# Order of products in a four-layer kernel: output tiles, a g tile inside the third mixer, a value tile, and small products between quarter tiles

## The chip, the core and the metric

One core of a Trainium2 chip runs the whole program in one launch. The metric is the device time of one execution in microseconds (us). TensorE (PE in the rows) multiplies, VectorE (DVE), ScalarE (ACT) and GpSimd (POOL) prepare its operands and take its results, and SyncE (SP) issues the loads of the weights from HBM.

## The reference, cut to what matters

Two models of two layers each run one after the other on one activation of 256 tokens by 1024 features, in float32.

```python
def fox_mixer(h, ...):      # attention, 16 heads of 64, with a forget gate of 16 columns
    q, k, v, f, z = split(h @ w_in);  log_f = log_sigmoid(f + b_f);  c = cumsum(log_f)
    ...
    return (o * silu(z)) @ w_out
def nsa_mixer(h, ...):      # q, kc, vc, ks, vs, kw, vw, gate, z = split(h @ w_in)
    kc = compress_blocks(kc_raw, pe_k, w_ck1, w_ck2)   # blocks of 32 tokens @ w1, silu, @ w2
    ...
    return (o * silu(z)) @ w_out
def _hgrn2_mixer(h, ...):   # third mixer: q, f, i, g = split(h @ w_in), 8 heads of 128
    o = _chunk_gated_recurrence(silu(q), 1 - forget, i, log(forget))
    return (_rmsnorm(o, out_norm) * silu(g)) @ w_out
...
def second_block(...):      # per layer: x += mixer(rmsnorm(x)); x += conv_ffn(rmsnorm(x))
```

The order is fox mixer, nsa mixer, hgrn mixer, FFN, MLA mixer, FFN.

## The kernel before, in words

**Weights.** All weights pass through a ring of three slots as tiles of 1 MB (128 partitions x 2048 float32). For each tile SP loads the ring slot, ACT writes the high part (`high`, line 385), DVE subtracts to get the low part (`low`, line 395, or in halves, line 404), and PE forms each product as three matmuls, high*high, low*high and high*low (`product3`, lines 421 to 423). SP may load tile t when the low part of tile t-3 is made; ACT may write the high part of tile t when PE has finished tile t-3. The list `tiles` sets the order, and every engine's program names the tiles in that order.

**A tile on PE.** `by_feature` and `by_token` do one tile as 2 halves (j) of 8 chunks (c) of 3 matmuls, 48 matmuls of 256 columns, into one of the PSUM banks 0 and 1, in turn. A bank is free when the tile two before it has been taken by DVE or ACT (`wait_bank`). `between(q)` is called after each quarter of a tile (4 chunks, 12 matmuls) and can put other products there. `ready(c)` waits for chunk c of the activations.

**Output projections.** `project_out` does the four tiles of the fox, nsa, hgrn and MLA output projections. In its first tile each chunk of half j=0 waits for `act_split`, the count of activation chunks that are split in high and low. In the fox, nsa and hgrn mixers the last two chunks come from the mixer's last z or g tile: DVE takes the bank, ACT applies tanh or silu, DVE multiplies, ACT writes the high part, DVE the low part (lines 1501, 1956, 2368).

**Fox.** The forget gate's product of 16 columns (`forget_product`, line 1391, 16 calls of two instructions each) is done at once in the middle of tile 1.

**NSA.** Tile order: kc, vc, ks, vs, kw, hk0, vw, hk1, q0, hv0, ... where hk and hv are the tiles of the compression's first product (`hidden`). They need the token blocks that DVE builds (`blocks`, line 1903, then the copy of line 1984 and the subtraction of line 1986, `block_split`) after eight DMAs have moved rows. DVE's order there is low(kw), wait for the DMAs, blocks(0), rope(0), blocks(1), high and low parts of the blocks, low(hk0), low(vw), low(hk1), rope(1), ... The second operation of rope(0) (line 1893) frees the bank of tile ks, which is the bank that kw needs.

**Third mixer.** After the f, q and i tiles comes a core of 8 heads. For each head PE sums exponents with the `levels` matrices (`exponents`, lines 2117 and 2119; w = 2*head + half, into banks 0 and 1 for an even w and 2 and 3 for an odd one), ACT takes exp (line 2221), DVE multiplies 8 levels (`mix`, line 2323), PE forms scores (`scores`, lines 2131 to 2139), DVE masks (2331) and adds levels (2339), PE forms outputs (`outputs`, lines 2150 to 2155, into bank 7 alone, one head after the other), ACT copies them out and squares them (2240, 2242). Then PE does g tile 0, 16 sums of squares (line 2171, each two instructions with one column), g tile 1, four spreads of the inverted roots (line 520), and g tiles 2 and 3.
DVE's queue behind g tile 1, in order: take g tile 1 (line 2269), norm and gate of parts 0 and 1, norm of parts 2 and 3 (line 2356; part i waits for spread i), low of output tile 0 (line 395), output_low(0) and (1) (line 2368), take g tile 2, gate(2), output_low(2), low of output tile 1, take g tile 3, gate(3), output_low(3). ACT's queue at its end: silu(2), output_high(2), high of output tile 1, silu(3), output_high(3).

## Time and profile before

| what | us |
|---|---|
| three runs | 1115.91, 1118.05, 1108.06 (median 1115.91) |
| the profiled execution's own time | 1112.2 |
| its span in the profile | 1110.4 |
| PE busy in the span | 1058.5 |
| DVE busy | 770.7 |
| ACT busy | 548.7 |

The profiled execution stands at 1112.2 us, of which 1.8 us lie around the span; it is 3.7 us below the median of the three runs. PE's busy time counts an engine that runs at half clock as fully busy, so the granted clock is read beside it.

### The profile page before, as it was taken

To read this page: it belongs to the slowest core of one execution; us is meant where nothing else is said; L and a number is where in the kernel's file an instruction comes from. 1 tells how busy PE (TensorE), PEld (TensorE's weight loads), DVE (VectorE), ACT (ScalarE), POOL (GpSimd) and SP (SyncE) were. 2 spreads that over 40 slices of the span, in tenths; PEclk is the share of its full clock that TensorE was granted. 3 is DMA by queue.
4 is the path that set the end of the run, shared out by engine and by line. 5 is a ranking of instruction groups with operands and counts; after the bars stand their busy time and mean duration, and the time that the engine had idled before them with its cause. 6 is when DMAs were issued, how large, how long until landed. Compare 5 with 4: busy or idle time off the path is not lost. (4 is left out here: it accounts for less than half of the span.)

```text
span 1110.4 us, 20549 instructions
## 1 busy us (share of the span) xinstructions
PE 1058.5 (95%) x8304; PEld 993.9 (90%) x8306; DVE 770.7 (69%) x1276; ACT 548.7 (49%) x862; POOL 76.5 (7%) x60
## 2 busy tenths in 40 slices
PE   7999999999998999899999999999899899999997
PEld 5988889897676999898989999999888799999997
DVE  5666666767676667477456887787677548887875
ACT  5544445355555545543355544454564455544451
POOL 4000005000000410000011000000300320000000
PEclk9899999999999999999999999999999999999999
DMA  8544335782112446400345666664323045755641
GB/s 265 152 120 147 115 117 171 223 265 75 39 39 77 149 155 194 148 1 7 104 130 141 190 193 178 195 188 144 120 76 115 19 134 153 216 171 180 189 152 39
DMA packets 176974, 152.31 MB, mean 137 GB/s; under 512 B 6845, under 2 KB 169220, under 8 KB 176900
## 3 DMA queue, kind: packets, MB, share of 16 engines
q1 hardware_dynamic: 176690, 151.22, 45.0%
q8 instruction: 52, 0.85, 0.3%
q14 instruction: 22, 0.18, 0.1%
q10 hardware_dynamic: 210, 0.05, 0.0%
HBM read 148.12 MB, written 1.05 MB: 134 GB/s over the span
## 5 line engine op out<-in xcount | busy, mean ns | idle before, releaser
L421 PE MATMUL bank<-h_high,w_high 128*128 128x256 f32 x1312 | 381.9, 291 | 6.2 <-DVE ffn_normed L1040 2.6
L422 PE MATMUL bank<-h_low,w_high 128*128 128x256 f32 x1312 | 374.0, 285 | 0.0
L423 PE MATMUL bank<-h_high,w_low 128*128 128x256 f32 x1312 | 373.8, 285 | 0.0
L385 ACT ACTIVATE w_high<-ring 128x2048 fp32r<-128x2048 f32 x138 | 263.3, 1911 | 189.1 <-PE bank L423 181.9
L395 DVE TENSOR_TENSOR w_low<-ring,w_high 128x2048 fp32r<-128x2048 f32 x119 | 273.4, 2300 | 32.6 <-ACT w_high L385 32.4
L421 PEld LDWEIGHTS bank<-h_high,w_high 128*128 128x128 f32 x1312 | 254.4, 194 | 13.5 <-issue 8.3
L422 PEld LDWEIGHTS bank<-h_low,w_high 128*128 128x128 f32 x1312 | 254.6, 194 | 0.7 <-issue 0.5
L423 PEld LDWEIGHTS bank<-h_high,w_low 128*128 128x128 f32 x1312 | 254.5, 194 | 0.0
L421 PE MATMUL bank<-ffn_hidden_high,w_high 128*128 (+1 forms) x352 | 99.8, 283 | 2.0 <-DVE ffn_hidden_low L1073 2.0
L422 PE MATMUL bank<-ffn_hidden_low,w_high 128*128 (+1 forms) x352 | 99.6, 283 | 0.0
L423 PE MATMUL bank<-ffn_hidden_high,w_low 128*128 (+1 forms) x352 | 99.6, 283 | 0.0
L568 POOL TENSOR_TENSOR h<-h 128x512 f32<-128x512 f32 x18 | 43.7, 2427 | 713.9 <-ACT h L552 713.3
L1049 DVE SCALAR_TENSOR_TENSOR ffn_conv<-ffn_normed,par,ffn_conv 128x254 f32<-128x254 f32 (+1 forms) x176 | 77.0, 479 | 7.4 <-ACT ffn_conv L1027 2.3
L1027 ACT ACTIVATE ffn_conv<-ffn_normed,par 128x256 f32<-128x256 f32 x88 | 48.0, 593 | 67.4 <-DVE ffn_normed L1040 67.2
L744 ACT ACTIVATE work<-bank,work 128x128 f32<-128x128 f32 (+1 forms) x112 | 46.2, 418 | 60.6 <-DVE work L729 60.5
L421 PEld LDWEIGHTS bank<-ffn_hidden_high,w_high 128*128 128x128 f32 x352 | 67.6, 192 | 2.3 <-issue 2.3
L423 PEld LDWEIGHTS bank<-ffn_hidden_high,w_low 128*128 128x128 f32 x352 | 67.6, 192 | 0.0
L422 PEld LDWEIGHTS bank<-ffn_hidden_low,w_high 128*128 128x128 f32 x352 | 67.6, 192 | 0.0
L729 DVE TENSOR_REDUCE work<-bank 128x2 f32<-128x256 f32 (+2 forms) x64 | 32.4, 507 | 40.0 <-PE bank L715 39.8
L710 PE MATMUL bank<-work 128*128 128x256 f32 (+2 forms) x160 | 53.2, 432 | 1.9 <-DVE work L2718 1.5
L404 DVE TENSOR_TENSOR w_low<-ring,w_high 128x1024 fp32r<-128x1024 f32 x38 | 46.1, 1220 | 7.1 <-ACT w_high L385 7.0
L421 PE MATMUL bank<-w_high,h_high 128*128 128x256 f32 x160 | 47.5, 297 | 2.9 <-DVE w_low L395 2.9
(344 smaller groups left out, 1823.9 us busy)
## 6 DMA issues: line engine op xcount, KB each, us to landing
ring<-in_ffn_w_up_dram SPq DMA_DIRECT2D x44, 1024.0 KB, 6.0
ring<-in_ffn_w_down_dram SPq DMA_DIRECT2D x22, 1024.0 KB, 5.0
ring<-in_fox_w_in_dram SPq DMA_DIRECT2D x16, 1024.0 KB, 5.7
ring<-in_hgrn_w_in_dram SPq DMA_DIRECT2D x16, 1024.0 KB, 5.5
ring<-in_nsa_w_in_dram SPq DMA_DIRECT2D x14, 1024.0 KB, 5.4
ring<-in_fox_w_out_dram SPq DMA_DIRECT2D x4, 1024.0 KB, 5.1
ring<-in_nsa_w_out_dram SPq DMA_DIRECT2D x4, 1024.0 KB, 5.1
ring<-in_hgrn_w_out_dram SPq DMA_DIRECT2D x4, 1024.0 KB, 5.2
```

Of the source, the lines that this page charges most:

```text
L385: i = nc.scalar.activation(dst, src, ACT.Copy)
L395: ops.tensor_tensor(w_lo[:, t % NSLOT, :], ring[:, t % NSLOT, :], w_hi[:, t % NSLOT, :].bitcast(F32), ALU.subtract).then_inc(low_in[t % NS ...
L404: i = nc.vector.tensor_tensor(w_lo[:, t % NSLOT, q], ring[:, t % NSLOT, q], w_hi[:, t % NSLOT, q].bitcast(F32), ALU.subtract)
L421: nc.tensor.matmul(o, ah, bh, start=start, stop=False, **kw)
L422: nc.tensor.matmul(o, ah, bl, start=False, stop=False, **kw)
L423: return nc.tensor.matmul(o, al, bh, start=False, stop=stop, **kw)
L568: nc.gpsimd.tensor_tensor(h[:, 0:2, :], h[:, 0:2, :], h[:, 2 * i:2 * i + 2, :], ALU.add).then_inc(n_added, 1)
L710: nc.tensor.matmul(o, q, k, start=(i == 0), stop=False)
L729: nc.vector.tensor_reduce(self.least[:, m, 0:unit["nh"]], self.bank(u), AX.X, ALU.min).then_inc(a_least, 1)
L744: i = nc.scalar.activation(pb[:, e, 0:unit["w"]], ps[:, e, :], ACT.Exp, scale=-1.0, bias=self.least[:, m, e:e + 1], accum_out=self.sum[:, ...
L1027: i = nc.scalar.activation(y[:, j % 2, e, :], un[:, j % 2, e, :], ACT.Identity, scale=column(cw + 4 * FC, e, j, later), bias=column(cb, e, ...
L1049: i = nc.vector.scalar_tensor_tensor(out=dst, in0=un[:, j % 2, e, 0:S - back], scalar=column(cw + (2 - back) * 2 * FC, e, j, later), in1=d ...
```

## The change

- Output tiles: a new `by_feature_late` does the first tile of each `project_out` with chunks 0 to 5 of half j=0, chunks 0 to 5 of half j=1, then chunks 6 and 7 of both.
- Fox: `forget_product` is cut in three parts of 6, 5 and 5 calls, put after quarters 0, 1 and 2 of tile 1.
- NSA: tile vw goes ahead of hk0 in the ring, on PE and on ACT. On DVE the low part of tile 5 of the mixer (now vw) goes ahead of the wait for the moved blocks; that of tile 6 (now hk0) stays behind the blocks, and that of tile 7 goes behind rope(1).
- Third mixer: at the start of the core w = 1 goes ahead of w = 0, only w = 0 waits for the banks of the i tiles, and ACT makes one small Exp ahead of its last i tile; every one of DVE's 8 multiplications of a head signals by itself, and each pair of score products waits for its own level; g tile 0 goes between the last scores and the outputs of heads 6 and 7; the sums of squares are cut in three parts after quarters 0, 1 and 2 of g tile 1; the four spreads go after the four quarters of g tile 2.

The queues of DVE and ACT behind the core are as before.

```diff
@@ -295,8 +295,8 @@
         nsa("ks", NSA_KS)
         nsa("vs", NSA_VS)
         nsa("kw", NSA_KW)
+        nsa("vw", NSA_VW)
         nsa_hidden("hk0", 0)
-        nsa("vw", NSA_VW)
         nsa_hidden("hk1", 1)
@@ -496,6 +496,21 @@
                         between(2 * tt + c // 4)
+        def by_feature_late(pe, t, act, ready):
+            in_parts(pe, t)
+            wait_bank(pe, t)
+            w = parts(t, "p (c n) -> p c n", c=DC, n=256)
+            for chunks in (range(DC - 2), range(DC - 2, DC)):
+                for j in range(2):
+                    for c in chunks:
+                        if j == 0:
+                            ready(c)
+                        mm = product3(pbank(t)[:, j * S:(j + 1) * S], [v[:, c, j * P:(j + 1) * P] for v in w],
+                                      [v[:, c, :] for v in act], (j, c) == (0, 0), c == DC - 1, skip_group_check=True)
+            mm.then_inc(tile_done, 1)
@@ -893,8 +908,9 @@
             first = first(nrm)
 
             def pe(pe):
-                for t in range(t0, t0 + 4):
-                    by_feature(pe, t, split, ready=(lambda c: pe.wait_ge(act_split, n0 + c + 1)) if t == t0 else None)
+                by_feature_late(pe, t0, split, lambda c: pe.wait_ge(act_split, n0 + c + 1))
+                for t in range(t0 + 1, t0 + 4):
+                    by_feature(pe, t, split)
                 first(pe)
                 nrm.sums(pe)
@@ -1384,20 +1400,19 @@
 
-                def forget_product():
+                def forget_product(part):
                     pe.wait_ge(w_f_ready, 1)
-                    for tt in range(TT):
-                        for c in range(DC):
-                            mm = nc.tensor.matmul(B[6][:, tt * FOX_H:(tt + 1) * FOX_H], x[:, c, tt * P:(tt + 1) * P],
-                                                  w_f[:, c, :], start=(c == 0), stop=(c == DC - 1))
-                    mm.then_inc(fps, 1)
+                    for i in range((0, 6, 11)[part], (6, 11, 16)[part]):
+                        tt, c = i // DC, i % DC
+                        mm = nc.tensor.matmul(B[6][:, tt * FOX_H:(tt + 1) * FOX_H], x[:, c, tt * P:(tt + 1) * P],
+                                              w_f[:, c, :], start=(c == 0), stop=(c == DC - 1))
+                    if part == 2:
+                        mm.then_inc(fps, 1)
 
                 def between(n, half):
 
-                    if (n, half) == (1, 0):
-                        forget_product()
                     if (n, half) == (2, 0):
                         c_sums()
                 def quarter(n, q):
                     if (n, q) == (1, 0):
                         nrm_fox.spread(pe)
+                    if n == 1 and q < 3:
+                        forget_product(q)
                     if q % 2:
                         between(n, q // 2)
@@ -1780,8 +1797,8 @@
                 by_feature(pe, NT2["ks"], hsp)
                 by_token(pe, NT2["vs"], hsp, between=rotate_after(0))
                 by_feature(pe, NT2["kw"], hsp)
+                by_token(pe, NT2["vw"], hsp, between=rotate_after(1))
                 hidden("hk0", 0, 0)
-                by_token(pe, NT2["vw"], hsp, between=rotate_after(1))
                 hidden("hk1", 0, 1)
@@ -1842,8 +1859,8 @@
                 evac_raw("ks", raw_k[0])
                 evac_values("vs", v2[0])
                 evac_raw("kw", raw_k[1])
+                evac_values("vw", v2[1])
                 hidden_in("hk0", 0, False)
-                evac_values("vw", v2[1])
                 hidden_in("hk1", 0, True)
@@ -1975,6 +1992,7 @@
                 lowest = pc("lower", 0, DC)
                 nc.vector.tensor_tensor(lower_exp[:, :], lowest, lowest, ALU.subtract).then_inc(lb_step, 1)
                 low(dve, nc.vector, t_in + 4)
+                low(dve, nc.vector, t_in + 5)
                 dve.wait_ge(moved_x, 128)
                 dve.wait_ge(nsa_cleared, XB_CLEAR)
                 blocks(0)
@@ -1985,10 +2003,9 @@
                 dve.wait_ge(block_high, 1)
                 nc.vector.tensor_tensor(b_lo[:, :, :], xb, b_hi[:, :, :].bitcast(F32),
                                         ALU.subtract).then_inc(block_split, 1)
-                for t in range(t_in + 5, t_in + 8):
-                    low(dve, nc.vector, t)
+                low(dve, nc.vector, t_in + 6)
                 rope(1)
-                for t in range(t_in + 8, t_in + 13):
+                for t in range(t_in + 7, t_in + 13):
                     low(dve, nc.vector, t)
                 rope(2)
                 low(dve, nc.vector, FIRST + 1)
@@ -2104,13 +2121,14 @@
                     by_token(pe, t_i + i, hsp)
                 pe.wait_ge(lf_split, 4)
                 pe.wait_ge(levels_in, 1)
-                evacuated(pe, t_i + 2)
-                evacuated(pe, t_i + 3)
 
                 def exponents(w):
                     hh, tt = w // 2, w % 2
+                    if w == 0:
+                        evacuated(pe, t_i + 2)
+                        evacuated(pe, t_i + 3)
                     if w >= 2:
-                        pe.wait_ge(decayed, w - 1)
+                        pe.wait_ge(decayed, max(2, w - 1))
                     for b in range(2):
                         c0 = 512 * (1 + tt) if b else 0
@@ -2123,14 +2141,15 @@
                 def scores(w):
                     hh, tt = w // 2, w % 2
                     tk = slice(tt * P, (tt + 1) * P)
-                    pe.wait_ge(mixed, hh + 1)
                     if w >= 2:
                         pe.wait_ge(masked, w - 1)
                     d = dec[:, hh % 2]
                     for l in range(MASKED):
+                        pe.wait_ge(mixed, (LEVELS + 1) * hh + l + 1)
                         nc.tensor.matmul(B[4 + tt][:, l * HD:(l + 1) * HD].rearrange("p (b i) -> p b i", i=1 << l),
                                          d[:, l, tk], halves(d[:, l, tk], l)[:, :, 1, :], start=True, stop=True)
                     nc.tensor.matmul(B[4 + tt][:, MASKED * HD:], keyT[:, hh, tk], qT[:, hh, tk], start=True, stop=True)
+                    pe.wait_ge(mixed, (LEVELS + 1) * (hh + 1))
                     if hh and not tt:
                         pe.wait_ge(cross_in, hh)
 
                 for k in range(HG_H + 2):
                     if k < HG_H:
-                        exponents(2 * k)
-                        exponents(2 * k + 1)
+                        exponents(2 * k + (k == 0))
+                        exponents(2 * k + (k > 0))
                     if 1 <= k <= HG_H:
                         scores(2 * k - 2)
                         scores(2 * k - 1)
+                    if k == HG_H:
+                        pe.wait_ge(decayed, NU)
+                        by_feature(pe, t_g, hsp)
                     if k >= 2:
                         outputs(k - 2)
 
-                by_feature(pe, t_g, hsp)
-                pe.wait_ge(sq_in, HG_H)
-                for k in range(NU):
-                    mm = nc.tensor.matmul(B[2][:, k:k + 1], sq8[:, k // 2, k % 2 * P:(k % 2 + 1) * P], ones[:, 0:1],
-                                          start=True, stop=True)
-                mm.then_inc(sq_ps, 1)
-                by_feature(pe, t_g + 1, hsp)
-                pe.wait_ge(o_inv, 1)
-                for i in range(4):
-                    spread(B[3 + i], [roots[:, k:k + 1] for k in range(4 * i, 4 * i + 4)]).then_inc(o_spread, 1)
-                by_feature(pe, t_g + 2, hsp)
+                def square_sums(q):
+                    pe.wait_ge(sq_in, HG_H)
+                    for k in range((0, 5, 10, NU)[q], (5, 10, NU, NU)[q]):
+                        mm = nc.tensor.matmul(B[2][:, k:k + 1], sq8[:, k // 2, k % 2 * P:(k % 2 + 1) * P],
+                                              ones[:, 0:1], start=True, stop=True)
+                    if q == 2:
+                        mm.then_inc(sq_ps, 1)
+                def spread_roots(q):
+                    pe.wait_ge(o_inv, 1)
+                    spread(B[3 + q], [roots[:, k:k + 1] for k in range(4 * q, 4 * q + 4)]).then_inc(o_spread, 1)
+                by_feature(pe, t_g + 1, hsp, between=square_sums)
+                by_feature(pe, t_g + 2, hsp, between=spread_roots)
                 by_feature(pe, t_g + 3, hsp)
                 out3_pe(pe)
@@ -2204,6 +2229,8 @@
                     half = slice(i % 2 * 512, (i % 2 + 1) * 512)
                     nc.scalar.activation(lf_hi[:, i // 2, half], B[2 + i][:, :], ACT.Copy).then_inc(lf_high, 1)
                 for i in range(4):
+                    if i == 3:
+                        nc.scalar.activation(scratch[:, :], eps[:, :], ACT.Exp)
                     act.wait_ge(tile_done, t_i + i + 1)
                     for tt in range(TT):
@@ -2214,7 +2241,7 @@
 
                 def exps(w):
                     hh, tt = w // 2, w % 2
-                    act.wait_ge(summed, w + 1)
+                    act.wait_ge(summed, w + 1 if hh else 2 - w)
@@ -2224,8 +2251,8 @@
 
                 for k in range(HG_H + 3):
                     if k < HG_H:
-                        exps(2 * k)
-                        exps(2 * k + 1)
+                        exps(2 * k + (k == 0))
+                        exps(2 * k + (k > 0))
                     if k == 1:
                         high(act, t_g + 2)
@@ -2320,8 +2347,7 @@
                     dve.wait_ge(decayed, 2 * hh + 2)
                     for l in range(LEVELS + 1):
                         d = halves(dec[:, hh % 2, l, :], l)
-                        i = nc.vector.tensor_tensor(d, d, sources(hh, l), ALU.mult)
-                    i.then_inc(mixed, 1)
+                        nc.vector.tensor_tensor(d, d, sources(hh, l), ALU.mult).then_inc(mixed, 1)
```

## Rows read from the trace of the kernel before

**Rows 1.** Page, part 1, busy time, share of the span and instructions of each engine

```profile
PE 1058.5 (95%) x8304; PEld 993.9 (90%) x8306; DVE 770.7 (69%) x1276; ACT 548.7 (49%) x862; POOL 76.5 (7%) x60
```

**Rows 2.** Windows: stretch, length, busy time (instructions) by engine, granted PE clock, DMA

```profile
31.99:37.80 5.81, 5.81 (x28) 5.81 (x29) 0.89 (x4) 2.08 (x4) 0.00 (x0) 0.50 0.56 172
460.90:475.00 14.10, 11.06 (x68) 9.10 (x68) 8.57 (x24) 10.08 (x17) 0.00 (x0) 1.00 0.22 75
640.00:660.00 20.00, 20.00 (x169) 20.00 (x168) 16.05 (x23) 8.96 (x10) 0.00 (x0) 1.00 0.69 199
```

**Rows 3.** Timeline of PE, first fox output tile: start, length, instruction, [idle before]

```profile
149.42 0.28 PE L421 MATMUL bank<-fox_out_high,w_high 128*128 128x256 f32 x1
...
151.43 0.27 PE L423 MATMUL bank<-fox_out_high,w_low 128*128 128x256 f32 x1
154.15 0.58 PE L421 MATMUL bank<-fox_out_high,w_high 128*128 128x256 f32 x1 [2.44 <-DVE fox_out_low L1501]
```

**Rows 4.** Waits of PE over the span: total us, times, longest

```profile
PE bank L421 <- DVE w_low L395: 5.7, 3, 2.9
...
PE bank L421 <- DVE blocks_low L1956: 3.4, 1, 3.4
...
PE bank L421 <- DVE hgrn_out_low L2368: 2.6, 1, 2.6
...
PE bank L421 <- DVE fox_out_low L1501: 2.4, 1, 2.4
...
PE bank L2131 <- DVE work L2323: 1.8, 1, 1.8
...
PE bank L421 <- POOL mla_out_low L439: 1.4, 1, 1.4
...
PE bank L2117 <- ACT work L2209: 1.0, 1, 1.0
PE bank L2150 <- DVE work L2339: 1.0, 1, 1.0
```

**Rows 5.** Groups of PE instructions: the forget product

```profile
L1391 PE MATMUL bank<-w_f,x 128*128 128x16 f32 x32 | 4.1, 276 | 0.0
```

**Rows 6.** Timeline of DVE in the NSA mixer, tiles ks to hk0

```profile
198.76 1.89 DVE L1903 TENSOR_TENSOR work<-work,par 128x480 f32<-128x480 f32 x2 [2.10 <-DMA work<-work]
...
201.16 0.68 DVE L1893 TENSOR_TENSOR work<-bank,work 128x512 f32<-128x512 f32 x1
...
205.83 2.29 DVE L1986 TENSOR_TENSOR blocks_low<-work,blocks_high 128x2048 fp32r<-128x2048 f32 x1
```

**Rows 7.** Timeline of ACT over the same stretch

```profile
196.34 1.90 ACT L385 ACTIVATE w_high<-ring 128x2048 fp32r<-128x2048 f32 x1
202.45 0.84 ACT L1808 ACTIVATE work<-bank,rstd 128x256 f32<-128x256 f32 x2 [4.22 <-PE bank L423]
```

**Rows 8.** Timeline of ACT, start of the third mixer's core

```profile
461.89 1.28 ACT L2221 ACT_TABLE_LOAD   x1
```

**Rows 9.** Timeline of DVE, first heads of the third mixer

```profile
465.43 5.59 DVE L2323 TENSOR_TENSOR work<-work 128x256 f32<-128x256 f32 x16 [5.18 <-ACT work L2221]
```

**Rows 10.** Timeline of PE, sums of squares and spreads of the roots

```profile
532.71 3.66 PE L2171 MATMUL bank<-cst,work 128*128 128x1 f32 x32
...
543.54 3.73 PE L520 MATMUL bank<-cst,work 128*128 128x128 f32 x32
```

**Rows 11.** Timeline of DVE, end of the third mixer

```profile
547.40 1.52 DVE L2356 SCALAR_TENSOR_TENSOR h<-h,par,bank 128x512 f32<-128x512 f32 x2
548.96 2.29 DVE L395 TENSOR_TENSOR w_low<-ring,w_high 128x2048 fp32r<-128x2048 f32 x1
...
553.06 0.69 DVE L2269 TENSOR_TENSOR work<-bank,rstd_row 128x512 f32<-128x512 f32 x1 [0.60 <-PE bank L423]
...
562.81 0.69 DVE L2368 TENSOR_TENSOR hgrn_out_low<-h,hgrn_out_high 128x512 fp32r<-128x512 f32 x1 [0.82 <-ACT hgrn_out_high L2251]
...
568.90 0.69 DVE L906 TENSOR_TENSOR x<-bank,x 128x512 f32<-128x512 f32 x1 [2.07 <-PE bank L423]
```

## The prediction

> **What bounds the kernel.** The page's first part comes first [rows 1]: PE is busy for 1058.5 of 1110.4 us, DVE for 770.7 and ACT for 548.7, so PE's order of work sets the end, and a microsecond is won only where PE waits or runs slowly. Two views show where that is. In the windows the steady pace is 169 products in 20 us, 0.118 us each, at a granted clock of 1.00 (the 2.4 GHz level); at 31.99 it is 0.50 (1.2 GHz), and 28 products take 5.81 us [rows 2]. The reader is to see that PE counts as fully busy there too. I read the same 0.50 at 154.0, 212.0, 362.3, 526.0, 536.3, 563.8 and 792 us, each for 3.1 to 3.4 us, behind a wait of PE or behind tiny products. The waits of PE are the second view: eight rows hold nearly all that this change touches [rows 4].
>
> **Price of a half-clock stretch.** At 5.81 / 28 = 0.2075 us each, 3.3 us hold 16 products that need 1.9 at full pace: 1.4 us [rows 2]. A whole tile under it gives more: between the end of the sums of squares (532.71 + 3.5) and the spreads at 543.54 lie 7.3 us for 48 products that take 5.7, so 1.6 us [rows 10]. I take 1.5.
>
> **Forget product.** 32 instructions of 16 columns take 4.1 us in one piece [rows 5], and the 5.81 us behind them hold 28 products that need 3.3 [rows 2]: 2.5 us lost. In three pieces of 12, 10 and 10 instructions with quarters of 12 full products (1.4 us) between them, the tiny products keep their 4.1 us, and the 2.5 come back if the clock stays up. The sum that DVE waits for (its next tile take and low part are queued behind) is ready some 1.5 us later, at 33.5, but tile 1 still ends after it, near 35, and the cumulative sums are wanted only three us later. Bounds: 0 and 2.5; I take 2.5, since even one quarter between pieces gives PE as much full work as tiny work.
> The Trainium skill, "TensorE: Matmul & The Clock Gate", section "Why this matters for your kernels", ties a drop to idle gaps between bursts of matmuls. Here the list of waits has none in front of 31.99, yet the clock is 0.50; by the page the split would return nothing, and the sum would be 2.5 us smaller.
>
> **Output tiles, four times.** The fox tile starts at 149.42, its 18th product starts at 151.43 and the next at 154.15, when the last low part is there [rows 3]. With 18 products of the other half moved ahead (18 x 0.118 = 2.1 us) the wait of 2.4 becomes 0.3 to 0.5, and the stretch at 154.15 goes: 2.1 + 1.5 = 3.6 us. At the nsa output the wait is 3.4 [rows 4]; 1.3 is left, less than the 1.8 behind which the first scores ran at a clock of 1.00 [rows 2], so 3.6 again. At the MLA output the wait is 1.4, with no half clock: 1.4 us. The hgrn output is below. For the price of a wait that is already fulfilled, the 18 products of rows 3 serve: a wait stands before every third one, and 17 steps in 2.01 us are 0.118 each, as without waits. It is nothing.
>
> **Value tile ahead of the blocks.** PE waits 2.2 us for hk0's low part (in the first row of rows 4), which DVE makes only after the blocks' low part at 205.83 + 2.29 [rows 6], and a half-clock stretch follows (212.0). With vw's 48 products (5.7 us) between, both go: 3.7 us. But DVE's low part of vw now stands ahead of the blocks. It can start when ACT's high part ends, 196.34 + 1.90 [rows 7], and takes 2.3 us [rows 11]: 200.5. The blocks started at 198.76, so everything behind them shifts by 1.75 us: the second operation of rope(0), which frees the bank that kw needs, ends at 201.16 + 0.68 + 1.75 = 203.6 instead of 201.84 [rows 6]. PE is ready for kw at 202.3 (ACT takes the tile before it at 202.45 [rows 7]), so a new wait of 1.3 us arises there. hk0 then has 5 us to spare. On SP the load of vw takes hk0's place ahead of the eight block moves, and the load that waits for tile 5's low part goes out at 200.5 instead of 210.3, so no load is late. Net 2.2 + 1.5 - 1.3 = 2.4 us; between 0.9 (a half clock stays) and 3.7.
>
> **Start of the third mixer's core.** PE waits 1.0 us for ACT's last i tile and 1.8 us for DVE's first eight multiplications [rows 4]. Afterwards w = 1 fills the first wait, and ACT's table load of 1.28 us [rows 8] lies ahead of the last i tile. Both exps end 1.3 us earlier, so DVE's multiplications, 0.35 us each (5.59 us for 16 [rows 9]), start near 464.2. PE waits for both exps once (1.1 us) and reaches the scores at 466.1, level by level behind DVE, instead of 468.3. Gain 2.2 us; bounds 1.3 (if PE must wait for the last level) and 2.8.
>
> **g tile 0 before the last outputs.** It covers the 1.0 us wait for head 7's scores [rows 4]. Two outputs then follow each other in bank 7, and the second waits for ACT's copy of the first: 0.5 us. Two half-clock tiles (526.0 and 536.3), the second behind 32 one-column instructions of 3.66 us [rows 10], cost 1.6 each. With the sums cut up I count both as returned: 0.5 + 3.2 = 3.7 us, lower bound 0.5.
>
> **Spreads between the quarters of g tile 2.** This is the place that speaks against the change. Call T the start of the spreads, 543.54 [rows 10]. All four were done by T + 3.7; DVE did norms 2 and 3 at T + 3.9, the next low part at T + 5.4, took g tile 2 at 553.06 = T + 9.5 and ended the last low part of the output at 562.81 + 0.69 = T + 20.0; the first hgrn output tile was taken at 568.90 = T + 25.4 [rows 11]. In the changed kernel g tile 2 starts at T, and spread 3 is over only at T + 4 x 1.42 + 4 x 0.93 = T + 9.4. Norm 3 is queued on DVE ahead of all the rest: norm to 10.2, low part (2.29) to 12.5, two output lows (1.28) to 13.8. Then g tile 2 is taken, 4.3 us late, and the chain from there, 10.4 us [rows 11], ends at T + 24.2. PE comes to the late chunks at T + 20 (9.4 + 5.7 + 36 x 0.118, and 0.9 for chunk 4), waits 4 us, has a half clock, and ends the tile at 24.2 + 1.4 + 1.4 = T + 27.0. That is 1.6 us later than before. Were the spreads done at once, it would end at T + 21.4, so their place costs 5.6 us.
>
> **The sum.** 2.5 + 3.6 + 2.4 + 3.6 + (2.2 + 3.7 - 1.6) + 1.4 = 17.8 us. The profiled execution, 1112.2 us, becomes 1094.4; it lies 3.7 below the median of the three runs, which would become 1098.1. The four executions average 1113.6 us, so I predict 1096. These four spread over 10 us, 0.9%; about 1% is what a measurement can tell from no change.
>
> **Rivals.**
> *DVE has more room than I count* (0.10). If rope(0) or norm 3 were not late, 1.3 + 5.6 come on top: 24.7 us, 1089. Against it: DVE's rows are in the order of its program throughout [rows 6, 11].
> *The clock stays down* (0.23). Tiny products between quarters and the waits left could still be followed by 1.2 GHz. The stretches in my sum are worth 2.5 + 1.5 + 1.5 + 1.5 + 3.2 = 10.2 us; if none comes back, 7.6 are left, 1106; if half, 1101. For it: two outputs, a wait and the cut sums now stand in one row after g tile 0. Against it: the first scores' clock of 1.00 [rows 2].
> *The one-piece rule* (0.05). If tiny products never lower the clock and something else did at 31.99 and 536.3, the forget split and the split sums return nothing: 2.5 + 1.6 less, 1100. Against it: both stretches begin with the pieces [rows 2, 10]. This is what the rule of the Trainium skill's page named above would give.
> *Slower, by the waits in the scores* (0.03). Each of 16 calls has six more waits, 96 in all. If one between short products cost 0.3 us, as it might if it kept the next weights from being loaded early, 29 us are added: 1125. It decides from 17.8 / 96 = 0.19 us each. Against it: 0.00 in rows 3.
> *My forecast* (0.59): 1090 to 1102 by its own bounds.
>
> **How the numbers follow.** Faster by over 1% needs 11 us: nearly all of the forecast, the first rival, half of the second and most of the third, 0.80. Slower by over 1% is the fourth, 0.03; 0.17 is left for within 1%. The range of 8 in 10 reaches from 1087 (the first rival on the lower of the four executions' bases) to 1107 (no clock back).
>
> **What would show it.** Granted clock near 1.00 at 31 to 38 and in the first fox and nsa output tiles; a new PE wait of 1 to 1.5 us at the start of kw for rope(0)'s second operation; the first L2131 some 2 us earlier against the i tiles; the wait for L2368 at the hgrn output larger than its 2.6 us of before, near 4, with 0.50 behind it; no wait at the MLA output. The prediction is wrong if half-clock stretches appear inside tile 1 of fox or g tile 1, or if the L2368 wait has shrunk to under 1 us.

## Result and the profile after

The changed kernel takes 1096.95 us (median of six, 1094.86 to 1098.95) against 1114.05 us of the kernel before on the same chip (1108.06 to 1120.3): ratio 0.9855, 95% interval 0.9817 to 0.9893. The forecast was 1096, with a range of 1087 to 1107. The profiled execution took 1094.86 us, with a span of 1093.1. In later runs the kernel before was timed 46 times more, beside the experiments, and the 7 slow ones, over 1.5% above the fastest of their group, are left out of its means below and kept only where its scatter is told.

The page's first part, the changed kernel (against [rows 1], PE's busy time is 10.4 us shorter; it has two records more, but the weight loads, 8306, are the same, so the products are too; DVE and ACT are as before):

```profile
PE 1048.1 (96%) x8306; PEld 984.1 (90%) x8306; DVE 770.4 (70%) x1276; ACT 548.9 (50%) x863; POOL 76.5 (7%) x60
```

The waits of PE over the span (line, what released it: total us, times, longest), to be read against [rows 4]:

```profile
PE bank L421 <- DVE hgrn_out_low L2394: 4.5, 2, 3.7
PE bank L421 <- DVE w_low L395: 3.5, 2, 2.9
...
PE bank L421 <- DVE work L1910: 1.3, 1, 1.3
...
PE bank L421 <- DVE blocks_low L1973: 1.2, 1, 1.2
...
PE bank L2135 <- ACT work L2248: 1.2, 1, 1.2
PE bank L2169 <- ACT h L2267: 0.6, 1, 0.6
```

What was 3.4 at the nsa output is 1.2; the fox output's 2.4 is 0.3; the MLA output's 1.4, the scores' 1.8 (L2131) and the 1.0 ahead of the last outputs (L2150) are gone; so are 2.2 of the w_low row (hk0). New are 1.3 in front of kw (L1910, rope(0)'s second operation), 1.2 for both exps (L2135, in place of 1.0 for ACT's last i tile) and 0.6 for ACT's copy (L2169). The wait at the hgrn output grew from 2.6 to 4.5.

The windows of the same profile (stretch, length, busy time and instructions by engine, granted clock, DMA): the fox tile with the forget product, the core's start, and the first hgrn output tile.

```profile
29.00:37.00 8.00, 8.00 (x71) 8.00 (x70) 4.12 (x7) 4.57 (x5) 0.00 (x0) 1.00 0.44 133
...
452.00:468.00 16.00, 16.00 (x117) 14.66 (x115) 14.01 (x40) 9.56 (x17) 0.00 (x0) 1.00 0.01 2
...
547.00:555.00 8.00, 5.82 (x28) 5.82 (x29) 4.64 (x6) 5.22 (x6) 0.00 (x0) 0.57 0.56 153
```

Of the stretches at 0.50 listed in the prediction this profile has one, at 776 (792 before); one near 16 stands in both profiles (17 before) and is not in that list. A new one of double length begins at 547.8, inside the grown wait (545.5 to 549.2), and lasts to 554.6. Where the time came from, by the starts of the same instructions in the two profiles:

| up to | before | after | gained in the section |
|---|---|---|---|
| cumulative sums of fox | 40.39 | 36.92 | 3.5 (0.4 of it lay ahead of tile 1) |
| NSA rotate products | 198.52 | 191.54 | 3.5 |
| NSA gate product | 242.20 | 232.76 | 2.5 |
| behind the nsa output's four tiles | 384.15 | 371.07 | 3.6 |
| first scores of the third mixer | 468.32 | 453.27 | 2.0 |
| T, the end of g tile 1 (the spreads before, g tile 2 after) | 543.54 | 524.99 | 3.5 |
| behind the hgrn output | 585.98 | 570.38 | -3.0 |
| end of the span | 1110.4 | 1093.1 | 1.7 |

### The profile page after: what moved, and what is told of

It reads as the page before. It is cut to its first block and busy times, and to the rows that moved or that the text cites. A ratio compares the mean times of both kernels' runs of the same rounds, so it can differ in the third digit from the quotient of the medians.

```text
span 1093.1 us, 20559 instructions
## 1 busy us (share of the span) xinstructions
PE 1048.1 (96%) x8306; PEld 984.1 (90%) x8306; DVE 770.4 (70%) x1276; ACT 548.9 (50%) x863; POOL 76.5 (7%) x60
## 5 line engine op out<-in xcount | busy, mean ns | idle before, releaser
L421 PEld LDWEIGHTS bank<-h_high,w_high 128*128 128x128 f32 x1312 | 251.6, 192 | 15.0 <-issue 9.8
L422 PEld LDWEIGHTS bank<-h_low,w_high 128*128 128x128 f32 x1312 | 251.9, 192 | 0.7 <-issue 0.5
L423 PEld LDWEIGHTS bank<-h_high,w_low 128*128 128x128 f32 x1312 | 251.8, 192 | 0.0
```

The lines of the kernel that those rows point to most:

```text
L421: nc.tensor.matmul(o, ah, bh, start=start, stop=False, **kw)
L422: nc.tensor.matmul(o, ah, bl, start=False, stop=False, **kw)
L423: return nc.tensor.matmul(o, al, bh, start=False, stop=stop, **kw)
```

## Two parts of a time

Each run gives its span and its mean granted clock. Span times clock is roughly what the span would be at 2.4 GHz throughout; I call it the full-clock time, and the remainder the clock loss. It is an approximation (half clock under a wait costs nothing but is counted), with a use: from run to run of one kernel the full-clock time varied by 0.3 to 1.1 us (standard deviation), while the 46 runs of the kernel before reach from 1104.3 to 1123.7 us. The scatter is in the clock. Medians of the times, and means of the two parts:

| kernel | runs | median us | full-clock | clock loss |
|---|---|---|---|---|
| before | 39 | 1115.3 | 1093.4 | 18.1 |
| changed | 6 | 1096.9 | 1086.0 | 9.1 |
| spread_once | 6 | 1092.3 | 1082.1 | 8.7 |
| norm_later | 4 | 1096.7 | 1083.6 | 11.2 |
| rope_first | 4 | 1095.9 | 1086.3 | 8.2 |
| forget_one | 4 | 1097.8 | 1086.1 | 10.1 |
| late_only | 10 | 1101.5 | 1085.9 | 14.9 |
| order_back | 10 | 1103.2 | 1088.3 | 13.0 |
| more_waits | 4 | 1096.9 | 1086.2 | 8.8 |
| late_spread | 6 | 1100.2 | 1084.2 | 14.5 |
| spread_norm | 6 | 1095.2 | 1082.1 | 10.6 |
| g_back | 4 | 1100.1 | 1086.4 | 11.8 |
| both_once | 4 | 1097.6 | 1083.0 | 12.9 |

A difference between two full-clock means has a standard error of 0.3 to 0.6 us, one between two means of the clock loss 0.7 to 1.6 us. So a full-clock difference counts from about 1 us on, a difference in clock loss only from 2 to 3 us on. The experiments ran on three chips, where the kernel before had full-clock means of 1093.2, 1093.4 and 1093.5 us, so the chip doesn't explain the rows.

The change brought 7.4 us in work and waits and 9.0 us in clock. The prediction's sum of 17.8 held 7.6 us outside half-clock stretches and 10.2 in them.

The table shows one thing that the sum of 17.8 hides. late_only has the output tiles alone, and its full-clock time, 1085.9, is that of the whole change, 1086.0. All the other edits together brought nothing in work and waits that can be told from noise: what the value tile, the core's start and g tile 0 gained there, the place of the spreads took back. They brought clock, 14.9 against 9.1, a difference of 5.7 us with a standard error of 1.5. The prediction's terms say the same once they are put in this order: outside half clock, 2.1 + 2.1 + 1.4 at the fox, nsa and MLA outputs and 2.1 more at the hgrn output, if nothing stood against it, make 7.7; 0.9 + 2.2 + 0.5 - 1.6 for the rest, less these 2.1, leave -0.1.

## Experiments

All start from the changed kernel, unless said. None leaves out or changes part of the computation.

**spread_once.** The four spreads in one piece ahead of g tile 2.

```diff
-                by_feature(pe, t_g + 2, hsp, between=spread_roots)
+                for q in range(4):
+                    spread_roots(q)
+                by_feature(pe, t_g + 2, hsp)
```

> The changed kernel with the four spreads in one piece ahead of g tile 2. My theory (they hold back norm 3 and with it DVE's queue): the two waits for hgrn_out_low, 0.8 + 3.7 us, shrink to one under 1 us, both half-clock stretches behind them go, and the time falls by 6 to 7 us against the changed kernel, to a ratio of about 0.979 to the kernel before. Rival (the last g tile's own chain of DVE and ACT sets the end of the wait, wherever the spreads stand): the wait stays over 3 us and the time within 1.5 us of the changed kernel.

1092.26 us (1090.07 to 1095.42; ratio to before 0.9824, 0.9773 to 0.9874); five of its six runs lie below the fastest of the changed kernel. The median fell by 4.7 us and the mean by 4.4, where 6 to 7 were expected. PE's timeline (start, length, instruction, idle before) has the spreads at T = 524.24 and a single wait in the hgrn output tile:

```profile
524.24 3.73 PE L535 MATMUL bank<-cst,work 128*128 128x128 f32 x32
...
544.27 0.39 PE L421 MATMUL bank<-hgrn_out_high,w_high 128*128 128x256 f32 x1 [0.46 <-DVE hgrn_out_low L2396]
```

In the changed kernel the same tile waits twice:

```profile
542.34 0.39 PE L421 MATMUL bank<-hgrn_out_high,w_high 128*128 128x256 f32 x1 [0.76 <-DVE hgrn_out_low L2394]
549.18 0.58 PE L421 MATMUL bank<-hgrn_out_high,w_high 128*128 128x256 f32 x1 [3.70 <-DVE hgrn_out_low L2394]
```

From T to the end of the hgrn output it is 38.8 us here (563.09 - 524.24) against 45.4 in the changed kernel. These 6.5 us between two profiles are 4.0 of waits and the double stretch of half clock. Over the runs it is 3.9 in full-clock time and only 0.4 in clock loss; the profile of spread_once has stretches that the changed kernel's lacks, at 789 and 836. The prediction gave the place of the spreads a cost of 5.6, of which 4.0 were waits and the rest clock: the waits came back, the clock did not in the mean. DVE's timeline in the changed kernel shows the chain it was worked from:

```profile
534.50 0.75 DVE L2382 SCALAR_TENSOR_TENSOR h<-h,par,bank 128x512 f32<-128x512 f32 x1 [1.64 <-PE bank L535]
535.28 2.29 DVE L395 TENSOR_TENSOR w_low<-ring,w_high 128x2048 fp32r<-128x2048 f32 x1
537.49 1.29 DVE L2394 TENSOR_TENSOR hgrn_out_low<-h,hgrn_out_high 128x512 fp32r<-128x512 f32 x2
538.70 0.68 DVE L2296 TENSOR_TENSOR work<-bank,rstd_row 128x512 f32<-128x512 f32 x1
...
548.43 0.69 DVE L2394 TENSOR_TENSOR hgrn_out_low<-h,hgrn_out_high 128x512 fp32r<-128x512 f32 x1 [0.83 <-ACT hgrn_out_high L2278]
...
552.38 0.68 DVE L922 TENSOR_TENSOR x<-bank,x 128x512 f32<-128x512 f32 x1
```

Norm 3 waits 1.64 us for the last spread and everything behind it on DVE is late: the take of g tile 2 at T + 13.7 (worked out: 13.8), the last low part done at T + 24.1 (24.2).

**norm_later.** On DVE, the low part of the next g tile and output lows 0 and 1 go ahead of norms 2 and 3.

```diff
-                output_norm(2)
-                output_norm(3)
                 low(dve, nc.vector, t_g + 4)
                 output_low(0)
                 output_low(1)
+                output_norm(2)
+                output_norm(3)
```

> The changed kernel with the spreads where they are, but DVE does norms 2 and 3 behind the low part of output tile 0 and the first two output lows. My theory (the order of DVE's queue is the cause): g tile 2 is taken at about T + 11.2 instead of T + 13.7, the long wait for hgrn_out_low falls from 3.7 to 1.0 to 1.5 us, the short one of 0.8 goes, and the time falls by 3 to 5 us. Rival (the spreads cost by themselves, as pieces between the quarters on PE): no more than 1 us is gained and the waits stay.

1096.69 us (1095.18 to 1097.92), the changed kernel's, where 3 to 5 less were expected. DVE took g tile 2 at T + 11.2, as expected. The wait went from 4.5 in two pieces to one, of 2.2 where 1.0 to 1.5 were expected:

```profile
549.22 0.39 PE L421 MATMUL bank<-hgrn_out_high,w_high 128*128 128x256 f32 x1 [2.19 <-DVE hgrn_out_low L2394]
```

Those 2.3 us are in the full-clock time (1083.6), and the clock loss was 2.1 larger in its four runs (standard error 1.0). It shows that DVE's queue behind norm 3 makes half of the wait; doing the spreads at once removes nearly all of it (spread_once). The cause of the larger loss stays open.

**spread_norm.** Both edits together.

> A candidate for a better version: the edits of spread_once and of norm_later together. Over its six runs spread_once had, by span times mean granted clock (the time that the span would have at full clock), 1082.1 us against 1086.0 of the changed kernel, and norm_later 1083.6. Both edits bring DVE to the takes behind the g tiles earlier, so their gains are largely the same one: theory, the wait of 0.5 us for the mixer's low part that spread_once still has goes and nothing else changes, 1091.5 to 1092. Rival: with the spreads done at once, norms 2 and 3 behind the low parts come late for output_low(2), and the wait grows to 1 or 2 us: 1093 to 1094.

1095.19 us (1090.16 to 1099.02), full-clock 1082.1, as spread_once: the two gains are one. The wait of 0.5 us did not go, so that part of the theory missed. The median is 2.9 us higher with the same full-clock time; the mean clock loss is 1.9 larger with a standard error of 1.6, which doesn't tell the two apart.

**both_once.** spread_once with the sums of squares in one piece too.

```diff
-                by_feature(pe, t_g + 1, hsp, between=square_sums)
+                for q in range(3):
+                    square_sums(q)
+                by_feature(pe, t_g + 1, hsp)
```

> spread_once with the sums of squares in one piece ahead of g tile 1 too, so that none of the small products of the third mixer is cut up. Theory by the prediction (a piece of 3.7 us of one-column products brings a half-clock stretch, 1.6 us): 1093.7 against 1092.3 of spread_once, with a granted clock of 0.50 inside g tile 1. Rival: the stretch does not come, or comes somewhere else instead, and the time is that of spread_once within 0.5 us; the full-clock time (span times mean clock) is 1082 in both cases.

1097.57 us (1096.56 to 1099.02), 5.3 above spread_once. Windows and PE's timeline:

```profile
514.00:530.00 16.00, 14.52 (x67) 13.67 (x68) 2.54 (x2) 7.07 (x10) 0.00 (x0) 0.57 0.35 115
```

```profile
518.16 6.98 PE L2193 MATMUL bank<-cst,work 128*128 128x1 f32 x32 [0.92 <-ACT work L2273]
```

The half clock came, but not as expected. It begins at 516.2, in the last outputs, 2 us ahead of the piece, where this kernel and spread_once issue the same products; these windows show it:

```profile
514.00:516.00 2.00, 1.44 (x8) 1.03 (x8) 0.00 (x0) 0.80 (x2) 0.00 (x0) 1.00 1.07 373
516.20:518.16 1.96, 1.04 (x4) 0.67 (x4) 0.00 (x0) 0.83 (x3) 0.00 (x0) 0.54 0.01 2
518.16:530.00 11.84, 11.84 (x55) 11.84 (x56) 2.54 (x2) 5.44 (x6) 0.00 (x0) 0.50 0.28 89
```

So this profile does not show the piece lowering the clock, only a clock that stays low over it, up to 530, so that the 32 one-column products took 6.98 us instead of 3.66 [rows 10]. What speaks for the cut is the sum over runs and profiles. The difference to spread_once is 0.9 us full-clock and 4.2 us clock (standard error 1.0). In the three other profiles with the sums in one piece (before, before_again, late_only) a stretch begins in the last microsecond of the piece. In ten profiles with the sums cut, none begins at them; but in three of these ten (forget_one, late_spread, spread_norm) a stretch from the last outputs or the start of g tile 1 runs on in that tile. The 0.9 us full-clock are the wait for the last squares, which the first quarter of g tile 1 hides when the sums are cut.

**g_back.** g tile 0 behind the last outputs again.

```diff
-                    if k == HG_H:
-                        pe.wait_ge(decayed, NU)
-                        by_feature(pe, t_g, hsp)
...
+                by_feature(pe, t_g, hsp)
                 by_feature(pe, t_g + 1, hsp, between=square_sums)
```

> The changed kernel with g tile 0 multiplied behind the last outputs again, as before (on PE alone; nothing else is moved). By the prediction's sum the tile's place covers 1.0 us of wait for head 7's scores against 0.5 us of new wait, and keeps up to two half-clock stretches away (1.6 us each). Theory: full-clock time 0.5 us longer (1086.5), and one stretch more in most executions, 1099. Rival: the cut sums of squares alone keep the clock up, and the tile's place is worth its 0.5 us only: 1097.5.

1100.09 us (1097.45 to 1102.43). The wait is back in PE's timeline:

```profile
510.79 0.61 PE L2169 MATMUL bank<-work 128*128 128x128 f32 x2 [0.96 <-DVE work L2363]
```

Full-clock 1086.4 against 1086.0, clock loss 11.8 against 9.1 (standard error 1.6), with 0.50 granted from 511.0 to 517.9, behind this wait. The 0.4 us in waits are as worked out. Whether the tile's place is worth clock as well stays open: two of the four runs lie at the rival's 1097.5, two near 1102.3.

**forget_one.** The forget product in one piece, as before.

```diff
-                    for i in range((0, 6, 11)[part], (6, 11, 16)[part]):
+                    for i in range(16):
...
-                    if n == 1 and q < 3:
-                        forget_product(q)
+                    if (n, q) == (1, 1):
+                        forget_product(0)
```

> The changed kernel with the forget product in one piece after quarter 1 of tile 1, as before. My theory (tiny products in one piece lower the clock): a granted clock of 0.50 for about 6.8 us behind it, with no wait of PE ahead of it, and the time 2.5 to 3 us above the changed kernel. Rival, the rule that only idle gaps lower the clock: the clock stays at 1.00 and the time is the changed kernel's.

1097.76 us (1097.34 to 1099.29), 0.8 above the changed kernel, where 2.5 to 3 were expected; the clock loss is 1.0 larger with a standard error of 0.7, so it is not told from none. Its profile has no half clock there; PE's timeline and the window:

```profile
26.38 3.64 PE L1407 MATMUL bank<-w_f,x 128*128 128x16 f32 x32
```

```profile
26.00:38.00 12.00, 12.00 (x105) 12.00 (x104) 7.89 (x15) 6.60 (x6) 0.57 (x1) 1.00 0.37 99
```

The same 32 products that in the profile before stood ahead of 5.81 us at 0.50 [rows 2] here stand ahead of full clock. The same holds in before_again and late_only, which also have the product in one piece: of four profiles one has the stretch. It is a matter of the execution, not of the product alone.

**before_again.** The kernel before, profiled a second time.

> The kernel before itself, once more, for a second profile of it. Theory: the waits of PE are the same to 0.1 us, and its half-clock stretches (at 17, 32, 154, 212, 362, 526, 536, 563 and 792 us in the first profile) are other ones in part, two or more gone or added, since its 40 runs so far reach from 1104 to 1123 us with mean clocks from 0.992 down to 0.974. Rival: the stretches sit behind the same waits and tiny products each time, and the spread of the runs has another source.

1111.21 us. Every wait of [rows 4] is there with the same length, within 0.2 us. The windows of its fox product, first fox output tile and first scores:

```profile
31.00:38.00 7.00, 7.00 (x60) 7.00 (x60) 3.85 (x8) 3.75 (x4) 0.00 (x0) 1.00 0.52 152
149.00:155.00 6.00, 4.25 (x36) 4.25 (x37) 3.33 (x4) 1.24 (x3) 0.00 (x0) 1.00 0.34 96
...
462.00:474.00 12.00, 10.21 (x53) 9.01 (x52) 8.01 (x23) 5.81 (x10) 0.00 (x0) 0.72 0.00 1
```

The stretches at 32 and 154 are gone, and a double one (466.8 to 473.6) came behind the 1.8 us wait for the first scores, where [rows 2] show 1.00. Those at 17, 207 (212), 357 (362), 524, 535, 562 and 791 came again.

**late_only.** From the kernel before, only `by_feature_late` and its call, as the diff of the change has them.

> The kernel before with one part of the change alone: the first tile of each of the three output projections multiplies its last two feature chunks last. Theory: the three waits of the PE for the low parts of the projections' inputs (3.4 and 2.4 us for the NSA and fox tiles, and what is left of 2.6 us for the mixer's) shrink to under 1.3 us each; with the half-clock stretch behind the fox tile this is worth 3.6 + 3.6 us, and up to 1 us at the mixer's, so 7 to 8 us of the before's time, ratio about 0.993. The forget product, the value tile and the start of the core still cost what they did before. Rival: the waits only move to another chunk, and the time is the before's.

1101.49 us (1098.33 to 1108.26), ratio to before 0.9904 (0.9865 to 0.9942). The full-clock time fell by 7.5 us: the four waits, 9.8 us in [rows 4], are 1.2 + 0.3 + 0.5 + 0, the last being the MLA output's, which has no row any more:

```profile
PE bank L421 <- DVE blocks_low L1972: 1.2, 1, 1.2
...
PE bank L421 <- DVE hgrn_out_low L2384: 0.5, 1, 0.5
...
PE bank L421 <- DVE fox_out_low L1517: 0.3, 1, 0.3
```

The waits are as by the theory. The clock loss fell by 3.2 as well (standard error 1.6), so the gain is above the 7 to 8 expected with the clock counted in. The rest of the loss stays: in this window PE has no idle time and yet a mean clock of 0.72. Its first stretch (516.5 to 519.9) follows a wait of 0.96 us that ended at 514.60; its second (526.8 to 533.6) begins at the end of the one-column products, with no wait since:

```profile
516.00:533.00 17.00, 17.00 (x109) 16.93 (x109) 3.90 (x4) 6.38 (x8) 0.00 (x0) 0.72 0.39 124
```

**order_back.** The value tile vw behind hk0 again.

```diff
+        nsa_hidden("hk0", 0)
         nsa("vw", NSA_VW)
-        nsa_hidden("hk0", 0)
...
+                hidden("hk0", 0, 0)
                 by_token(pe, NT2["vw"], hsp, between=rotate_after(1))
-                hidden("hk0", 0, 0)
...
+                hidden_in("hk0", 0, False)
                 evac_values("vw", v2[1])
-                hidden_in("hk0", 0, False)
```

> The changed kernel with the NSA value tile put back behind the block tile hk0 (in the order of the loads, of the PE and of the copies out). Theory: the PE waits for the rotated keys' and block parts again in front of hk0, about 2.2 us, and the 1.3 us in front of kw stays, so the gate product starts 2.2 to 2.5 us later and the time is 2 us longer than the changed kernel's, about 1099. Rival: DVE, which in the changed kernel takes the block parts earlier in its order, has them ready in time for the old place too, so that nothing is lost (within 0.5 us).

1103.24 us (1097.28 to 1108.38), full-clock 1088.3: 2.3 longer, the size of the theory. The places were wrong: DVE had the low part of hk0 in time, and that of hk1 was late. DVE's order was not put back (it names the tiles by their number), so this is not the order of before, and that the size agrees is in part luck. PE's timeline:

```profile
196.87 0.35 PE L421 MATMUL bank<-h_high,w_high 128*128 128x256 f32 x1 [1.32 <-DVE work L1910]
...
203.14 0.36 PE L421 MATMUL bank<-w_high,blocks_high 128*128 128x256 f32 x1 [0.29 <-DVE blocks_low L2004]
...
214.35 0.39 PE L421 MATMUL bank<-w_high,blocks_high 128*128 128x256 f32 x1 [1.57 <-DVE w_low L395]
```

The median rose by 6.3 us, and the clock loss by 3.9 (standard error 1.5), which the theory did not have.

**rope_first.** The low part of vw behind rope(0).

```diff
                 low(dve, nc.vector, t_in + 4)
-                low(dve, nc.vector, t_in + 5)
...
                 rope(0)
+                low(dve, nc.vector, t_in + 5)
                 blocks(1)
```

> The changed kernel with DVE's low part of vw behind rope(0) instead of ahead of the blocks. My theory (the low part delays the release of the bank of ks): the new wait of 1.3 us at the start of kw goes, nothing else appears, and everything behind is 1.3 us earlier. Rival (the moved blocks' DMAs are late by themselves, or the low part of vw becomes late): the 1.3 us stay or come back in front of vw or hk0.

1095.91 us (1095.11 to 1098.09), full-clock as the changed kernel's: a miss, and near the rival. The 1.3 us in front of kw are gone, and PE's timeline has 1.1 us in front of q0:

```profile
223.54 0.39 PE L421 MATMUL bank<-h_high,w_high 128*128 128x256 f32 x1 [1.06 <-DVE w_low L395]
```

SP loads q0's tile behind its wait for vw's low part; the load goes out at 198.66 in place of 193.61 in the changed kernel, so that what DVE does later there is late again three tiles on.

**more_waits.** Two fulfilled waits more ahead of each of the 96 small score products.

```diff
                         pe.wait_ge(mixed, (LEVELS + 1) * hh + l + 1)
+                        pe.wait_ge(levels_in, 1)
+                        pe.wait_ge(lf_split, 4)
```

> The changed kernel with two more semaphore waits, both long fulfilled, ahead of each of the 96 small score products (192 waits more). It computes the same. Theory: the PE takes a fulfilled wait while the product before it is still running, so the pace of the 6 products of a unit stays what it is in the changed kernel (about 0.12 us from one start to the next) and the time is the same, within 1 us. Rival, the slower case of the prediction: every wait costs the PE's queue some 0.1 to 0.3 us that shows between products, 192 of them up to 20 us and more; the changed kernel would then pay for its own 80 added waits too.

1096.93 us (1095.33 to 1097.76). The group of the small score products, changed kernel and then this one (busy time, mean ns of one, idle before):

```profile
L2149 PE MATMUL bank<-work 128*128 128x64 f32 x192 | 23.6, 272 | 0.0
```

```profile
L2151 PE MATMUL bank<-work 128*128 128x64 f32 x192 | 23.6, 272 | 0.0
```

192 waits changed neither figure; the fourth rival of the prediction is out. (The change itself added 96 waits, as the prediction counts, and not the 80 named above.)

**late_spread.** spread_once, and the first two tiles of each output projection take their last two chunks behind both tiles' first six.

```diff
-                by_feature_late(pe, t0, split, lambda c: pe.wait_ge(act_split, n0 + c + 1))
-                for t in range(t0 + 1, t0 + 4):
+                by_feature_late(pe, (t0, t0 + 1), split, lambda c: pe.wait_ge(act_split, n0 + c + 1))
+                for t in range(t0 + 2, t0 + 4):
```

> A candidate for a better version: the changed kernel with the four spreads in one piece ahead of the tile (the edit of spread_once) and with the first two tiles of each output projection, not one, taking their last two chunks behind both tiles' first six. Theory: spread_once is worth 4 us; of the waits that are left in front of the projections (1.25 us at the NSA one, 0.3 at the fox one, 0.5 at the mixer's) the second tile's six chunks (2.6 us of products) hide nearly all, worth about 1.8 us more, if no half-clock stretch is added. About 1090.5. Rival: the second tile's bank or its weights' parts aren't there in time, or the low parts are late for more than one chunk, so that the gain over spread_once is under 0.5 us, 1092 to 1093.

1100.22 us (1097.53 to 1103.91): a miss, 8 us worse than spread_once and beyond the rival too; 2.1 of them are full-clock time, the rest clock. The waits of PE for the low parts of the inputs are gone as expected, but tile 0 of the nsa output is taken 3.4 us later than in the changed kernel (358.02 against 354.58), of which 1.0 is how far the two profiles differ before it, and the tiles' takes and h_lows run up against each other at its end. DVE's timeline there, then PE's:

```profile
360.43 0.89 DVE L561 SCALAR_TENSOR_TENSOR h_low<-x,gain_hgrn,h_high 128x256 fp32r<-128x256 f32 x2 [1.72 <-ACT h_high L555]
...
368.97 2.96 DVE L561 SCALAR_TENSOR_TENSOR h_low<-x,gain_hgrn,h_high 128x256 fp32r<-128x256 f32 x2 [0.58 <-ACT h_high L555]
371.85 3.38 DVE L395 TENSOR_TENSOR w_low<-ring,w_high 128x2048 fp32r<-128x2048 f32 x1
```

```profile
376.94 0.58 PE L421 MATMUL bank<-h_high,w_high 128*128 128x256 f32 x1 [4.03 <-DVE h_low L561]
```

A pair of h_lows and a low part that otherwise take 0.89 and 2.29 us took 2.96 and 3.38 while POOL added squares beside them, ahead of the last take and the h_low that the next tile wants: a wait of 0.8 became 4.0, with half clock at 375.4 to 382.4 around its end. In the changed kernel one pair of h_lows is as slow (2.65 us at 372.55), but it is the last one, behind the last take.

## Why the prediction was right

The waits held step by step; the sum was 17.8 against 17.3 between the profiled spans and 16.4 between the means of the runs. That the sum came so near is in part luck, by the first and the last term below.

- *Forget product*, 2.5: 3.0 between the profiles. What goes beyond 2.5 is the product itself, which partly ran at half clock: 3.97 us from its start to the next product before, 3.33 in its three parts, where the prediction kept its 4.1. But the stretch stands in one of four profiles with the product in one piece, and between the runs the cut is worth 0.8 us, which their scatter doesn't tell from none (forget_one). The term was the price of one execution; for the mean it was too large.
- *Output tiles*, 3.6 + 3.6 + 1.4: 3.5, 3.6, and the MLA wait is gone (1.7 in the last section of the table). late_only isolates them: the waits fell by 7.8 us, hgrn output included, 7.5 in full-clock time. The half clock behind the fox wait was one execution's, though: in before_again it isn't there.
- *Value tile*, 2.4: 2.5, with the new wait at kw of 1.32 against 1.3 worked out. order_back gives 2.3 in full-clock time, by other waits than those of before.
- *Core start*, 2.2: 2.0. The scores follow level by level without a wait, PE waits 1.2 for both exps (1.1 worked out).
- *g tile 0 and the cut sums*, 3.7: 3.5 between the profiles; 0.6 of wait for ACT's copy (0.5 worked out). g_back finds 0.4 in waits and 2.7 in clock, which its scatter doesn't tell from none; both_once finds 0.9 and 4.2 for the cut of the sums.
- *Spreads between the quarters*, -1.6: -3.0. This term was mis-sized. Its chain on DVE was right to 0.1 us, and both pieces of the wait to 0.3, 0.76 + 3.70 where 0.9 (for chunk 4) and 4 were worked out. PE ended the tile at T + 26.9 (27.0 worked out), but the half clock was double (547.8 to 554.6, in place of 3.3 us) and reached over 13 products of the next tile, 1.2 us more. (By the prediction's own figures PE comes to the late chunks at T + 20.2, not T + 20, and the place costs 5.4 rather than 5.6.)

Of the rivals, more room on DVE fell: its rows came in the order of the program with the durations taken. The clock did come back, 9.0 us between the means where 10.2 were forecast. One thing in that argument was wrong though right by luck: a stretch at 0.50 was counted as belonging to its place ("a half-clock stretch follows"). before_again and forget_one show that it does so in some executions only. "The first scores' clock of 1.00" [rows 2], given as evidence that 1.8 us of wait leave the clock up, was one execution's; before_again has 0.50 there.

The one-piece rival is half right: forget_one's profile has no half clock behind the forget product in one piece, while the sums of squares in one piece cost 4.2 us of clock. And one sign that the prediction gave for being wrong, half clock inside g tile 1, is absent from the changed kernel's profile but there in those of forget_one, late_spread and spread_norm, with the sums cut. The rule weighed there (the Trainium skill, "TensorE: Matmul & The Clock Gate", section "Why this matters for your kernels", which ties a drop to idle gaps) does not cover the second stretch of late_only, from 526.8 on, where PE had not been idle since 514.60.

The change left something: its place for the spreads costs 3.9 us full-clock, and spread_once, with that one edit undone, is the fastest version measured, 1092.3 us (spread_norm has the same full-clock time and isn't told from it).

## What to carry to other kernels

Judge an edit by span times mean clock and by clock loss apart: the first repeats to within about a microsecond and shows a wait of 2 us in four runs, where the median time moved not at all (norm_later) or by 6 us (order_back). Before small products that another engine waits for are cut up to keep PE dense, follow what is queued behind that wait; cut those that nobody waits for soon (the sums), and do at once those that head a chain (the spreads). An input that comes late is covered by doing its chunks last in one tile, and here that alone was the whole gain in waits (late_only); over two tiles, the tile that the next stage wants first came late itself.

## What was not expected of the hardware

- The kernel before scatters over 19.4 us in 46 runs (mean granted clock 0.974 to 0.992), the changed one over 4.1 in six (0.990 to 0.993). That fewer waits and fewer rows of tiny products made the scatter smaller is not shown: spread_norm, with less waiting still, scatters over 8.9 us in six runs.
- Which places get the 1.2 GHz level differs between executions of one kernel with the same waits, and between near twins (spread_norm and spread_once). What decides it was not found; no experiment aimed at it alone.
- Where DVE and POOL ran side by side, one of the two was slow, now the one and now the other; no experiment aimed at it. In late_spread's profile POOL's addition at 365.67 took 3.27 us (its others there 1.3 to 1.5) beside a low part of 2.28, and then DVE's pair of h_lows took 2.96 instead of 0.89 beside POOL's two operations at 368.90 and 370.15, of 1.30 and 1.49.
- 32 one-column products took 3.66 us [rows 10], nearly all of it at full clock, and 6.98 at half: these tiny products slowed down with the clock too.
